# Six norms of a three-layer kernel: token sums over a stationary block of ones, root and reciprocal on 512 columns

## The reference

```python
def rms_norm(x, g):
    xf = x.astype(jnp.float32)
    y = xf * lax.rsqrt(jnp.mean(xf * xf, axis=-1, keepdims=True) + EPS)
    return (y * g.astype(jnp.float32)).astype(x.dtype)
```

## Time and profile before

| what | value |
|---|---|
| median of three runs | 2083.87 us |
| profiled execution, its own time | 2083.29 us |
| its span | 2081.5 us |
| mean granted TensorE clock | 0.997 |
| PE busy | 2043.9 us, 98% |
| DVE busy | 1084.2 us, 52% |
| ACT busy | 751.8 us, 36% |
| GpSimd busy | 228.2 us, 11% |
| DMA | 186.93 MB, mean 90 GB/s |

### The profile page before, as it was taken

The page is one execution under the profiler, slowest core; times in us unless marked ns, Lnnn a source line. Parts: engine busy times, 40 slices in busy tenths (PEclk is TensorE's granted clock), DMA queues, the critical chain, the costliest instruction groups (busy, mean ns, idle before and its releaser), DMA issues.

```text
span 2081.5 us, 27670 instructions
## 1 busy us (share of the span) xinstructions
PE 2043.9 (98%) x11217; PEld 1700.2 (82%) x11217; DVE 1084.2 (52%) x1388; ACT 751.8 (36%) x1041; POOL 228.2 (11%) x205
## 2 busy tenths in 40 slices
PE   7999999999999999999999999999999999999998
PEld 7887888888888888877888888888888778888886
DVE  4674765645344453354645444466775435344453
ACT  6434544422222332685422222232573333122221
POOL 3000222300000220001300000231302010000001
PEclk9999999999999999999999999999999999999999
DMA  6221002132222322102232222333222212222221
GB/s 253 81 101 61 22 23 82 61 122 82 99 101 101 119 71 94 41 1 102 78 105 98 85 99 101 122 122 123 90 82 101 81 59 83 101 101 90 93 99 61
DMA packets 28334, 186.93 MB, mean 90 GB/s; under 512 B 3537, under 2 KB 3665, under 8 KB 6481
## 3 DMA queue, kind: packets, MB, share of 16 engines
q1 hardware_dynamic: 25200, 173.48, 23.2%
q0 software_dynamic: 2320, 11.01, 1.5%
q10 hardware_dynamic: 720, 1.11, 0.2%
HBM read 181.39 MB, written 2.10 MB: 88 GB/s over the span
## 4 chain that ended last, share of the span: by engine, by line
PE 93%; DVE 3%; ACT 2%; DMA 1%; issue 1%; POOL 0%; ACTq 0%; DVEq 0%
PE PS L585 91%; ACT Y L1548 1%; DVE WL L2268 1%; DVE Y L2265 1%; ACT WH L1548 1%; DMA MX<-mem_t 0%; DMA STG<-weights 0%; PE PS L807 0%; PE PS L614 0%; DVE Y L2268 0%; ACT ABUF L1548 0%; DVE WT L2268 0%; POOL BT L518 0%; PE PS L955 0%; DVE SQ L2268 0%
## 5 line engine op out<-in xcount | busy, mean ns | idle before, releaser
L585 PE MATMUL PS<-HH,WH 128*128 128x512 f32 x1544 | 607.4, 393 | 3.0 <-DVE WL L2268 2.2
L585 PE MATMUL PS<-HH,WL 128*128 128x512 f32 x1544 | 601.2, 389 | 0.0
L585 PE MATMUL PS<-HL,WH 128*128 128x512 f32 x1544 | 590.6, 389 | 0.0
L1548 ACT ACTIVATE WH<-STG 128x2048 fp32r<-128x2048 f32 (+2 forms) x167 | 307.2, 1839 | 518.6 <-PE PS L585 516.4
L2268 DVE TENSOR_TENSOR WL<-STG,WH 128x2048 fp32r<-128x2048 f32 (+1 forms) x159 | 358.5, 2255 | 255.0 <-ACT WH L1548 254.9
L585 PEld LDWEIGHTS PS<-HH,WH 128*128 128x128 f32 x1544 | 289.9, 188 | 68.1 <-issue 5.0
L585 PEld LDWEIGHTS PS<-HH,WL 128*128 128x128 f32 x1544 | 289.9, 188 | 60.2
L585 PEld LDWEIGHTS PS<-HL,WH 128*128 128x128 f32 x1544 | 290.0, 188 | 59.6 <-issue 0.7
L585 PE MATMUL PS<-UPH,WH 128*128 128x512 f32 x832 | 324.2, 390 | 1.4 <-DVE UPL L2265 1.4
L585 PE MATMUL PS<-UPH,WL 128*128 128x512 f32 x832 | 323.7, 389 | 0.0
L585 PE MATMUL PS<-UPL,WH 128*128 128x512 f32 x832 | 323.7, 389 | 0.0
(11 more groups left out here) (321 smaller groups left out, 2042.4 us busy)
## 6 DMA issues: line engine op xcount, KB each, us to landing
STG<-weights SPq DMA_DIRECT2D x159, 1024.0 KB, 4.8
KEY_STG<-weights POOLq DMA_DIRECT2D x4, 1024.0 KB, 6.7
XT<-x_t SPq DMA_DIRECT2D x2, 1024.0 KB, 9.0
KEY_X<-mem_t POOLq DMA_DIRECT2D x2, 1024.0 KB, 6.6
out_t<-Y SPq DMA_DIRECT2D x8, 256.0 KB, 2.0
STG<-weights SPq DMA_DIRECT2D x4, 256.0 KB, 5.5
MX<-mem_t ACTq DMA_DIRECT2D x4, 256.0 KB, 7.7
CON<-consts SPq DMA_DIRECT2D x1, 1024.0 KB, 8.8
```

The source lines that it names most:

```text
L585: return pe.matmul(o, l, r, start=start, stop=stop, **kw)
L1548: return act.activation(o, i, f, **kw)
```

## The change

For six norms (A.in, A.mlp, B.mlp, C.in, C.cross, C.mlp) the sums come from one matmul with the 128x128 block of ones stationary and the 128x512 SQA moving, so that each of 128 partitions of bank 4 holds all 512 sums. ScalarE takes the root of 128x512 from that bank into the same bank, VectorE the reciprocal of 128x512 into RS. The transposes and the copy into RS are gone, RT and RSC are not written, and the counts of the semaphores `rsc` and `bc` leave these norms out. The orders on the engines stay.

```diff
--- before.py
+++ after.py
@@ -364,6 +364,7 @@
         ADDS = [6 if name in ("A.post", "A.post2", "B.post", "B.post2", "final") else 7 for name in SUMS]
         ADD_BASE = [sum(ADDS[:n]) for n in range(len(SUMS) + 1)]
         NORMS = [n for n in SUMS if n != "mem"]
+        WIDE = ("A.in", "A.mlp", "B.mlp", "C.in", "C.cross", "C.mlp")
 
         def score_at(c, b):
             return DF_OFF[b] + (0 if c == 0 else 256 if b == 1 else 1536)
@@ -371,11 +372,14 @@
         def sums_done(n):
             return SUMS.index(n) + 1
 
+        def inverted(n):
+            return sum(1 for x in SUMS[:sums_done(n)] if x not in WIDE)
+
         def bcast_done(n):
-            return NORMS.index(n) + 1
+            return sum(1 for x in NORMS[:NORMS.index(n) + 1] if x not in WIDE)
 
         def copies_done(n):
-            return sum(1 for x in NORMS[:bcast_done(n)] if x not in POSTS)
+            return sum(1 for x in NORMS[:NORMS.index(n) + 1] if x not in POSTS)
 
         def split_done(q, k):
             return 8 * SPLITS.index(q) + k + 1
@@ -595,6 +599,9 @@
                     pe.wait_ge(sems["rs"], copied)
                 if before and before[-1] in POSTS:
                     pe.wait_ge(sems["y_scaled"], 8 * POSTS.index(before[-1]) + KD)
+                if name in WIDE:
+                    mm(PS[:, 4, :], con("ones"), SQA[:, :], True, True).then_inc(sems["ss"], 1)
+                    return
                 for b in range(nt):
                     last = mm(PS[:, 4, b:b + 1], blk(SQA[:, :], b), con("ones")[:, 0:1], b == 0, alone,
                               skip_group_check=True)
@@ -609,7 +616,9 @@
 
             def spread_tokens(name, nt=NB):
 
-                pe.wait_ge(sems["rsc"], sums_done(name))
+                if name in WIDE:
+                    return
+                pe.wait_ge(sems["rsc"], inverted(name))
                 for b in range(nt):
                     last = pe.transpose(PS[:, 4, b * P:(b + 1) * P], RSC[:, b:b + 1].to_broadcast([P, P]), I_)
                 last.then_inc(sems["bc"], 1)
@@ -1583,9 +1592,14 @@
 
             def root(name, nt=NB):
                 act.wait_ge(sems["ss"], sums_done(name))
+                if name in WIDE:
+                    A(PS[:, 4, :], PS[:, 4, :], ACT.Sqrt, scale=1.0 / D, bias=EPST[:, 0:1]).then_inc(sems["sqrt"], 1)
+                    return
                 A(RT[:, 0:nt], PS[:, 4, 0:nt], ACT.Sqrt, scale=1.0 / D, bias=EPST[:, 0:1]).then_inc(sems["sqrt"], 1)
 
             def factor(name):
+                if name in WIDE:
+                    return
                 act.wait_ge(sems["bc"], bcast_done(name))
                 A(RS[:, :], PS[:, 4, :], ACT.Copy).then_inc(sems["rs"], 1)
 
@@ -1624,7 +1638,7 @@
                 if norm:
                     root(norm, MB)
                     split_hi(u + 2)
-                    act.wait_ge(sems["rsc"], sums_done(norm))
+                    act.wait_ge(sems["rsc"], inverted(norm))
                 for t in range(MB):
                     act.wait_ge(sems["tile"], 2 * u + t + 1)
                     A(dst(t), PS[:, 2 * (u % 2) + t, 0:UC], ACT.Copy, scale=RSC[:, t:t + 1]).then_inc(sems["emptied_act"], 1)
@@ -1971,7 +1985,7 @@
             split_hi(um + 3)
             stream_hi(4, KD)
             root("mem", MB)
-            act.wait_ge(sems["rsc"], sums_done("mem"))
+            act.wait_ge(sems["rsc"], inverted("mem"))
             memory_tiles(um, KR[0])
             memory_tiles(um + 1, V_MEM[0])
             split_hi(um + 4)
@@ -2122,7 +2136,7 @@
                     stick_log(1)
 
             act.preload_act_table_set("natural_log_exp_and_others")
-            act.wait_ge(sems["rsc"], sums_done("B.in"))
+            act.wait_ge(sems["rsc"], inverted("B.in"))
             memory_halves(1, MO, beside_memory)
             value_tiles(2, 1)
             stick_breaking()
@@ -2185,7 +2199,7 @@
 
             def memory_values(r):
                 act.wait_ge(sems["tile"], 2 * (R0["C.mem"] + r) + 2)
-                act.wait_ge(sems["rsc"], sums_done("mem2"))
+                act.wait_ge(sems["rsc"], inverted("mem2"))
                 for t in range(MB):
                     A(CV[:, t, UC * r:UC * (r + 1)], PS[:, 5, t * UC:(t + 1) * UC], ACT.Copy, scale=RSC[:, t:t + 1])\
                         .then_inc(sems["emptied_act"], 1)
@@ -2281,6 +2295,9 @@
 
             def invert(name, nt=NB):
                 dve.wait_ge(sems["sqrt"], sums_done(name))
+                if name in WIDE:
+                    dve.reciprocal(RS[:, :], PS[:, 4, :]).then_inc(sems["rs"], 1)
+                    return
                 dve.reciprocal(RSC[:, 0:nt], RT[:, 0:nt]).then_inc(sems["rsc"], 1)
 
             def units(name, norm=None, evac=None, behind=None, post=False):
```

## The result

Eight runs of the changed kernel took 2086.92 to 2095.4 us, median 2090.91; eight of the kernel before took 2083.2 to 2085.8, median 2083.91. The ratio is 1.0031, with a 95% interval of 1.0022 to 1.0040: 0.3% slower, where 0.17% was forecast. Besides the median the spread has changed, from 2.6 us to 8.5 us. The profiled execution took 2090.3 us, with a span of 2088.5 (2081.5 before).

A forecast was written before the change was run, and what follows sets the result against it. TensorE, busy 98% of the span, was taken as the bound. Losses of 4.77 us at A.mlp, B.mlp and C.in, 1.32 saved and 0.18 lost elsewhere gave +3.6 on 2083.87: 2087.5 us, range 2085.2 to 2090.6.

The forecast's parts named there:

- three waits: TensorE waiting on VectorE's reciprocal: 1.85 us lost in A.mlp, 1.53 in B.mlp, 1.39 in C.in.
- the sum: Whole kernel: 4.77 us lost at A.mlp, B.mlp and C.in, 1.32 saved and 0.18 lost elsewhere: +3.6 us.
- the prediction's own signs: Reciprocals near 3.4 us, TensorE waits of 1.8 us, about 0.5 us for WL in A.mlp, granted clock still 0.997.
- R: Time of the 128x512 reciprocal on VectorE in each of the six norms, taken as 3.4 us from narrow rows.
- Rival 1: Reciprocal dearer than its narrow rows, lengthening the waits in A.mlp, B.mlp and C.in: 3.8 us, total 2088.7; chance 0.24.
- rival 3: Reciprocal at the rate of VectorE's other operations, 0.69 us; all six norms save, total 2081.6 us; chance 0.04.
- The second wait in A.mlp: TensorE waiting for WL at the fourth unit in A.mlp, about 0.5 us.
- The unpaired places: A.in, C.cross, C.mlp: reciprocal hidden, 0.44 us saved on transposes and 0.06 lost on sums in each.
- The sums: On TensorE, one float32 matmul of 512 columns, 0.86 us, replaces four of one column, 0.80: 0.06 us more.
- rival 2: TensorE's clock falls after the new waits in A.mlp, B.mlp, C.in: one fall +5.3 us, three +8.7; chance 0.09.
- paired places: A.mlp, B.mlp, C.in: 12 matmuls between sums and transposes, 9 more before TensorE wants the bank; 4.77 us lost.
- One early wait of 1.98 us: TensorE's wait ending at 39.41 us, granted clock 1.00 behind it; a fall was taken to decide past 2 us.

The follow-up runs named there:

- e5_half: Changed kernel with the reciprocal on the first 256 columns only, the other 256 copied as the root; 2082.6 us, ratio 0.9996.
- e10_again: The changed kernel unedited, run once more; 2090.06 us.
- e4_copy: Changed kernel with VectorE copying the root into RS in place of the reciprocal, so the factor is wrong; 2079.47 us, ratio 0.9983.
- e8_lnexp: Changed kernel with ScalarE making the factor alone by Ln and Exp, no root and no reciprocal; 2079.54 us, ratio 0.9982.
- e7_fill3: Changed kernel with 3 extra, unread matmuls on TensorE during the wait in each of A.mlp, B.mlp and C.in; 2087.5 us.
- e2_paired: Changed kernel with only A.mlp, B.mlp and C.in wide, the other three norms narrow as before; 2089.5 us, ratio 1.0028.
- e1: Changed kernel with only A.in, C.cross and C.mlp wide, the other three norms narrow as before; 2083.11 us, ratio 0.9998.
- e9: Changed kernel with one more reciprocal of 192 columns, not read, ahead of RS in A.mlp, B.mlp and C.in; 2096.04 us.
- e3_fill: Changed kernel with 8 extra, unread matmuls on TensorE during the wait in each of A.mlp, B.mlp and C.in; 2087.79 us.

## Why the prediction was right, and where not

The price of the three waits was right; the clock behind them, which the sum puts at nothing, was not. So the forecast time is well off: 2087.5 us, 3.6 more than before, where the medians lie 7.0 apart. 2090.91 is 0.3 over the top of the range, 2090.6, and the ratio of 1.0031 on 2083.87 gives 2090.3, 0.3 under it: that this is so close to the range owes more to the room that it left for a dearer reciprocal than to its reasons. The likeliest outcome was to be no measurable change (0.62); it came out slower (0.35). Of the prediction's own signs the waits and the reciprocal came, the granted clock of 0.997 didn't (0.995), and A.mlp and B.mlp gave 3.05 and 3.15 us in the changed kernel's trace in place of 1.4 to 1.9.

**R.** 3.354 us against 3.4. With the widths of e5_half a column costs (3354 - 1754) / 256 = 6.25 ns, the slope of the narrow rows. By the Trainium skill, VectorE: DVE Perf Modes, the section on the fixed hardware budget, the divide has a repeat count of 8, from which the prediction made, at that page's 0.96 GHz, an estimate of 8.3 ns and R = 4.4; the page gives no cost for a column. The trace doesn't agree with the estimate: 6.25 ns are six such cycles, and the measurement decides. Rival 1 is out with it, and rival 3 as well.

**The three waits.** With R at its measured value the steps gave 1.80, 1.48 and 1.34 us (R less 1.55, 1.87 and 2.01). Where the clock stayed behind them the stages lost 1.82, 1.59 and 1.53 (e10_again). RR twice and UT once are what TensorE waited for, for 1.97 us each, where 1.8 had been expected. The second wait in A.mlp, for WL, is there and smaller than the 0.5 us foreseen. In e10_again WL ends at 416.72 + 2.29 = 419.01, and the fourth unit starts 0.47 us behind the matmul before it, 0.24 more than the ordinary distance:

```profile
418.59 0.39 PE L589 MATMUL PS<-HH,WL 128*128 128x512 f32 x1
419.06 0.50 PE L589 MATMUL PS<-HH,WH 128*128 128x512 f32 x1
```


**The unpaired places.** 0.38 us each had been expected; the changed kernel shows 0.20, 0.25 and 0.51. The sums were to cost 0.06 us more than before; by the rows of A.mlp they cost 0.05 less, the far end of what the prediction allowed. In A.in the read-out starts at 58.66, 7.44 us behind the sums, against 58.75 before, 7.71 behind them, so R hides as foreseen. What the steps missed is that the earlier factor is worth something there: e4_copy, e5_half and e8_lnexp gain 0.96 to 0.99. The wide reciprocal gives that back. Why A.in's stage is sensitive to it, and in steps, no run tells.

**The sum.** Over the six stages e10_again's execution lost 1.82 + 1.59 + 1.53 - 0.41 - 0.30 - 0.51 = 3.7 us; the prediction had 3.6. That is the fast end of what was measured (2086.55 to 2087.4 us), and e7_fill3, with the clock kept up, has its median at 2087.5.

**What failed** is the weight of rival 2, "TensorE's clock falls after the new waits", with a chance of 0.09 and the point from which it decides, "where a wait goes past 2 us". Behind waits of 1.96 to 1.98 us in the paired places the clock fell in four of nine cases: two of three in the changed kernel's trace, none in e10_again's, two in e2_paired's. Eight of 16 runs of the changed kernel have a granted clock of 0.994 to 0.996, which the traces show with two falls or more, and none of 67 runs of the kernel before that ran beside e1, e5 and e9. The argument against it, that hundreds of us of dense matmuls precede each place, was no protection. One early wait of 1.98 us without a fall had been read as a bound, where it was one draw: with 1.77 to 1.94 us the same wait has a fall behind it in three traces, and with 1.75 to 1.98 us none in four others. A fall costs 1.2 us in A.mlp (3.05 against 1.82), where part of it goes in front of the WL that would have been waited for anyway, and 1.6 us in B.mlp; 1.7 had been taken. The profiled execution adds up: its six stages give 3.05 + 3.15 + 1.54 - 0.20 - 0.25 - 0.51 = 6.8 us with two falls, of the 7.0 that it lies over the one of before. How many falls the run at the median had is not on record.

## What to carry to other kernels

Ask of a step that moves to an idle engine how long the engine that bounds the kernel will stand still for it, place by place: the same edit saved 0.2 to 0.5 us in three places and lost 1.5 to 3.2 in three others, because there 21 matmuls (4.8 us) and a split on VectorE lay between cause and need. Count a pause of the matmul engine of about two microseconds with the fall of its clock behind it, as a chance and not as a certainty, and expect the spread of the runs to grow. One place in one trace without a fall doesn't rule it out: look at the same place in several executions. And if an operation on 512 columns becomes the bound, ask which engine is idle at that moment: two activations of 0.6 us on ScalarE did the work of a reciprocal of 3.35 us on VectorE.

## What the runs showed of the hardware

A float32 reciprocal on VectorE costs 6.25 ns for each column (177 ns at 4, 1754 at 256, 3354 at 512), against 1.3 ns for a copy (688 ns at 512). The narrow widths were read from SBUF and the wide ones from PSUM, and one line fits both. One float32 matmul of 128x512 over ones takes the place of four of one column at about the same price: one record pair of 1.02 us against 0.95, and from the start of the sums to the second matmul behind them 1.09 us (398.17 to 399.26) against 1.14 before (398.18 to 399.32).

After an idle time of 1.97 us TensorE ran on at full speed for 1.2 us (405.97 to 407.2) and only then at half for 3.3 us, in some executions and not in others, at the same place and behind the same work. After one of 3.19 us its first matmul was already slow (0.77 us against 0.47) in two of three places. Matmuls that nobody reads, put into the pause, took the falls away in most runs. What decides a single fall stayed open, as did the two runs of e3_fill at 0.996, in which TensorE idled for 0.16 us at most in these places.
